# Feed-forward stages of a two-block transformer: output tiles placed between the block products, in six short stretches over a ring of eight tiles

## The reference

```
def swiglu(x, w_in, w_out):
    gate, up = jnp.split(x @ w_in, 2, axis=-1)
    return (jax.nn.silu(gate) * up) @ w_out

    x = x + FFN_HALF * rmsnorm(swiglu(rmsnorm(x, ffn1_pre_g), ffn1_w_in, ffn1_w_out), ffn1_post_g)
```

## Time and profile before

| | us |
|---|---|
| median of 2 runs | 3464.9 (3463.77 to 3466.04) |
| profiled execution, its own time | 3456.78 |
| its span in the profile | 3455.0 |

### The profile page before, as it was taken

The page is one execution under the profiler, slowest core; times in us unless marked ns, Lnnn a source line. Parts: engine busy times, 40 slices in busy tenths (PEclk is TensorE's granted clock), DMA queues, the critical chain, the costliest instruction groups (busy, mean ns, idle before and its releaser), DMA issues.

```text
span 3455.0 us, 50031 instructions
## 1 busy us (share of the span) xinstructions
PE 3112.0 (90%) x20476; PEld 2613.2 (76%) x20476; DVE 2193.9 (63%) x3116; ACT 1379.3 (40%) x2398; POOL 1493.2 (43%) x1003
## 2 busy tenths in 40 slices
PE   6999999899998989898899898997989999979897
PEld 4777778678776888876777788887888885678886
DVE  2256482446648696776554959679687616486967
ACT  3242273442454343442443434344233416452433
POOL 2234315235344474454212546427456343344743
PEclk9999999999999999998778999999999999999999
DMA  5213202212111222221001122231232230112222
GB/s 222 92 53 128 91 13 63 74 45 70 44 53 61 92 81 97 98 92 56 8 2 55 42 93 92 80 104 55 88 108 69 93 102 24 42 43 93 86 87 78
DMA packets 74164, 256.74 MB, mean 74 GB/s; under 512 B 8016, under 2 KB 11216, under 8 KB 72784
## 3 DMA queue, kind: packets, MB, share of 16 engines
q1 hardware_dynamic: 73072, 248.82, 21.3%
q0 software_dynamic: 864, 4.72, 0.4%
HBM read 251.41 MB, written 2.10 MB: 73 GB/s over the span
## 4 chain that ended last, share of the span: by engine, by line
PE 66%; DVE 19%; issue 5%; ACT 4%; POOL 4%; DMA 1%; SPq 0%; ACTq 0%; DVEq 0%; POOLq 0%
PE banks L459 64%; DVE area L1539 3%; DVE w_lo L436 3%; PE banks L468 2%; POOL w_lo L425 1%; ACT w_hi L409 1%; DVE area L1510 1%; POOL w_sum L447 1%; DVE area L1528 1%; DVE w_late L436 1%; DVE w_last L430 1%; DVE area L1517 1%; POOL w_sum L445 1%; DMA area<-in_w_mod 1%; DVE area L1534 0%
## 5 line engine op out<-in xcount | busy, mean ns | idle before, releaser
L459 PE MATMUL banks<-area,w_hi 128*128 128x256 f32 (+3 forms) x6892 | 1690.8, 337 | 154.1 <-DVE w_lo L436 120.7
L459 PEld LDWEIGHTS banks<-area,w_hi 128*128 128x128 f32 (+2 forms) x6892 | 1179.8, 191 | 335.4 <-DVE w_lo L436 134.3
L459 PE MATMUL banks<-area,w_lo 128*128 128x256 f32 (+3 forms) x3446 | 1140.8, 333 | 0.0
L459 PEld LDWEIGHTS banks<-area,w_lo 128*128 128x128 f32 (+2 forms) x3446 | 659.1, 191 | 69.8
L425 POOL TENSOR_TENSOR w_lo<-w_raw,w_hi 128x1024 fp32r<-128x1024 f32 (+2 forms) x146 | 344.8, 2363 | 517.1 <-ACT w_hi L409 479.5
L459 PE MATMUL banks<-area,w_late 128*128 128x256 f32 (+2 forms) x2766 | 499.1, 334 | 30.9 <-DVE w_late L436 29.3
L459 PEld LDWEIGHTS banks<-area,w_late 128*128 128x128 f32 (+1 forms) x2766 | 419.5, 192 | 92.7 <-DVE w_late L436 34.2
L459 PE MATMUL banks<-area,area 64*64 64x32 f32 (+11 forms) x4424 | 399.9, 314 | 65.9 <-DMA area<-in_w_mod 15.7
L459 PEld LDWEIGHTS banks<-area,area 64*64 64x64 f32 (+4 forms) x4424 | 308.7, 174 | 146.1 <-issue 57.9
L409 ACT ACTIVATE w_hi<-w_raw 128x1024 fp32r<-128x1024 f32 (+2 forms) x197 | 193.2, 985 | 321.3 <-PE banks L459 199.7
L436 DVE TENSOR_TENSOR w_lo<-w_sum,w_hi 128x1024 fp32r<-128x1024 f32 x115 | 207.1, 1803 | 47.1 <-POOL w_sum L450 42.4
(11 more groups left out here) (298 smaller groups left out, 4183.3 us busy)
## 6 DMA issues: line engine op xcount, KB each, us to landing
w_raw<-in_l_ffn_w_in SPq DMA_DIRECT2D x132, 512.0 KB, 3.4
w_raw<-in_w_in SPq DMA_DIRECT2D x66, 512.0 KB, 3.5
w_raw<-in_l_ffn_w_out SPq DMA_DIRECT2D x48, 512.0 KB, 3.5
const<-in_l_ffn_w_in SPq DMA_DIRECT2D x44, 512.0 KB, 3.5
w_raw<-in_w_mod SPq DMA_DIRECT2D x32, 512.0 KB, 4.6
w_raw<-in_w_out SPq DMA_DIRECT2D x32, 320.0 KB, 2.9
w_raw<-in_l_ffn_w_out SPq DMA_DIRECT2D x24, 384.0 KB, 3.2
w_raw<-in_w_qkv SPq DMA_DIRECT2D x18, 512.0 KB, 3.3
```

What stands on the lines that cost most here:

```text
L459: return e.matmul(out, lhsT, rhs, start=first, stop=stop, skip_group_check=True)
```

## The change

The stretches become 4, 4, 4, 4, 3, 3 tiles. The 8 output tiles of a stretch are no longer computed in a row but between the block products of the next stretch: `pairs_behind` gives each block one `w_out` piece (now two output tiles of 4 or 3 hidden tiles each; the last block of a three-block stretch has two pieces), and PE computes the first half of its output tiles between p6 and p7, the second half between p3 and p4. p4 stands in its own block. Blocks use banks 4-7 alone, output tiles banks 0-3. The hidden tiles lie in a ring of eight (`RING`). The output tiles of the last stretch follow all blocks, hidden tiles 19 and 20 first for four of them (`lead`). DVE takes out two tiles per block (`tiles_dve`), makes the rest of the `w_out` pieces between c11 and `a_lo_dve`, and takes over the rests that POOL had behind the stretches and of the first two pieces of the two mixers. ACT, DVE and POOL get the entries in a new order. The weight layout follows; the number of matmuls and bytes stays.

Lines that begin with a space stand in both kernels; "..." leaves lines out (in the ACT and DVE loops these are waits and signals).

```diff
-FFN_PHASES = ((0, 8), (8, 16), (16, 22))
+FFN_PHASES = ((0, 4), (4, 8), (8, 12), (12, 16), (16, 19), (19, 22))
+RING = 8
...
-            for p, (j0, j1) in enumerate(FFN_PHASES):
-                for c in range(2 * j0, 2 * j1):
+            for j in range(FT):
+                for c in (2 * j, 2 * j + 1):
                     yield (name + "_w_in", c, True)
-                for c in range(8):
+                for p, c in pairs_behind(j):
                     yield (name + f"_w_out{p}", c, True)
+            for c in range(4):
+                yield (name + f"_w_out{len(FFN_PHASES) - 1}", c, True)
+def pairs_behind(j):
+    p = next(p for p, (j0, j1) in enumerate(FFN_PHASES) if j0 <= j < j1)
+    if p == 0:
+        return []
+    i, n = j - FFN_PHASES[p][0], FFN_PHASES[p][1] - FFN_PHASES[p][0]
+    return [(p - 1, c) for c in range(4) if min(c, n - 1) == i]
...
-                    ents.append((n, "plain"))
-                    if ents[-2][1] == "s34":
-                        ents.append((ents[-2][0], "last"))
-                    ents += [(n, "s12"), (n, "s34")]
+                    ents += [(n, "plain"), (n, "s12"), (n, "s34"), (n, "last")]
             elif split:
-                after_units = len(ents) > 0 and ents[-1][1] == "s34"
                 ents.append((n, "whole"))
-                if after_units:
-                    ents.append((ents[-2][0], "last"))
         ent_at = {ent: k for k, ent in enumerate(ents)}
-        end_ents = {k + i for k, (n, kind) in enumerate(ents) if kind == "s34" and ents[k + 1][1] == "whole" for i in (1, 2, 3)}
...
-        last_leads = [n + i for n in firsts for i in (2, 3, 4, 5)]
+        last_leads = [n + i for n in firsts for i in range(6)]
...
-                if (kind == "whole" and dve == (("ffn" in order[m][0] or m in last_leads) and k not in end_ents)
+                if (kind == "whole" and dve == (m in last_leads or "ffn" in order[m][0])
                         or (kind == "plain" and not dve)):
...
-                if kind == "last" and dve == (k not in end_ents):
+                if kind == "last" and dve:
...
+                    final = p == len(FFN_PHASES) - 1
                     self.outs.append(ProjectOut(
-                        name, lambda m, p=p, n=j1 - j0: [(name + f"_w_out{p}", m, n)],
-                        [(self.a_hi[:, k, :], self.a_lo[:, k, :]) for k in range(j1 - j0)], T, y_sb, self.add.squares,
-                        lambda q, k, j0=j0: q.wait_ge(*at(name, "a", j0 + k)), add=p > 0, final=p == len(FFN_PHASES) - 1,
-                        free=lambda q, m, p=p: self.left_by_units(q, m, p), bank0=4 - 4 * self.bank_set(j1 - 1)))
-                assert self.outs[-1].bank0 == 0
+                        name, lambda m, p=p, n=j1 - j0: [(name + f"_w_out{p}", m // 2, n)],
+                        [(self.a_hi[:, j % RING, :], self.a_lo[:, j % RING, :]) for j in range(j0, j1)], T, y_sb,
+                        self.add.squares, lambda q, k, j0=j0: q.wait_ge(*at(name, "a", j0 + k)), add=p > 0, final=final,
+                        lead=[(m, k) for m in range(4) for k in range(j1 - j0 - 1)] if final else (),
+                        free=None if p else self.left_by_pieces, base=lambda m, n=j1 - j0: m % 2 * n))
...
-                return banks[self.quarter_bank(u, i)][:, 0:T // 2]
...
+                return banks[4 + i][:, 0:T // 2]
...
             def quarter_free(self, q, u, i):
...
+                if u > DIRECT:
                     q.wait_ge(*at(self.tag, self.LEFT_BY[i], u - 1))
...
                 else:
                     q.wait_ge(*at(self.tag, "x", "log", 0))
+            def tiles_behind(self, u, half):
+                tiles = [(p, m) for p, c in pairs_behind(u) for m in (2 * c, 2 * c + 1)]
+                n = len(tiles) // 2
+                return tiles[n:] if half else tiles[:n]
...
+                steps = [out.steps(q, e) for out in self.outs]
+                for u in range(DIRECT, FT):
+                    for name in ("p1", "p2", "p5", "p6"):
+                        self.product_pe(q, e, u, name)
+                    self.tiles_pe(steps, u, 0)
+                    for name in ("p7", "p3"):
+                        self.product_pe(q, e, u, name)
+                    self.tiles_pe(steps, u, 1)
+                    self.product_pe(q, e, u, "p4")
+                self.outs[-1].pe(q, e, steps[-1])
+            def tiles_pe(self, steps, u, half):
+                for p, m in self.tiles_behind(u, half):
+                    for _ in self.outs[p].k_tiles:
+                        next(steps[p])
...
+                if u >= RING:
+                    q.wait_ge(*at(*self.outs[self.phase(u - RING)].finished()))
+                e.activation(self.a_hi[:, u % RING, :], self.a[u % 2], ACT.Copy).then_inc(
...
+                for u in range(DIRECT, FT):
...
+                    e.activation(self.p1[u % 2], self.quarter(u, 0), ACT.Copy).then_inc(
...
+                    if u > DIRECT:
+                        self.a_hi_act(q, e, u - 1)
+                    else:
+                        for v in (0, 1):
+                            self.silu_act(q, e, v)
...
+                    e.activation(self.u2[u % 2], self.quarter(u, 0), ACT.Copy).then_inc(
...
+                    round_one(q, e, self.ent(u, "last"))
+                    if u == DIRECT:
+                        for v in (0, 1):
+                            self.a_hi_act(q, e, v)
+                        self.silu_act(q, e, 2)
+                    elif u + 1 < FT:
+                        round_one(q, e, self.ent(u + 1, "plain"))
+                    if u + 1 < FT:
+                        round_one(q, e, self.ent(u + 1, "s12"))
+                    else:
+                        round_one(q, e, self.last_ent())
+                    if u == DIRECT:
+                        self.a_hi_act(q, e, 2)
+                    self.silu_act(q, e, u)
+                    if u + 1 < FT:
+                        round_one(q, e, self.ent(u + 1, "s34"))
+                        for k in self.tile_ents(u + 1):
+                            round_one(q, e, k)
+                    else:
+                        round_one(q, e, self.last_ent() + 1)
+                self.a_hi_act(q, e, FT - 1)
+                self.final_act(q, e)
+            def after_ents(self):
+                return range(self.last_ent() + 4, ahead(ents[self.last_ent() + 3][0]) + 1)
+            def final_act(self, q, e):
+                out, after = self.outs[-1], list(self.after_ents())
+                q.w = self.last_ent() + 2
+                e.preload_act_table_set("natural_log_exp_and_others")
+                round_to(q, e, self.last_ent() + 3)
+                for k in after[:2]:
+                    round_to(q, e, k)
+                for m in range(DT - 1):
...
+                    out.squares.square(q, e, 0, m, out.y[:, m, :])
+                    if m >= 3:
+                        for k in after[m - 1:m]:
+                            round_to(q, e, k)
+                out.squares.last(q, e, 0)
...
+            def tiles_dve(self, q, e, u, half):
+                for p, m in self.tiles_behind(u, half):
+                    self.outs[p].evict(q, e, m, 0)
             def dve(self, q, e):
                 self.direct_dve(q, e)
...
+                for u in range(DIRECT, FT):
...
+                    if u > DIRECT:
+                        self.up_dve(q, e, u - 1)
+                        self.tiles_dve(q, e, u - 1, 1)
...
+                    e.tensor_tensor(self.half(sg, 0), self.quarter(u, 1), self.p1[u % 2], ADD).then_inc(
...
+                    for k in self.tile_ents(u):
+                        rest_one(q, e, k, dve=True)
+                    if u > DIRECT:
+                        self.a_lo_dve(q, e, u - 1)
+                        rest_one(q, e, self.ent(u, "s34"), dve=True)
...
+                    e.tensor_tensor(self.u4[u % 2], self.quarter(u, 2), self.u2[u % 2], ADD).then_inc(
...
+                    if u == DIRECT:
+                        rest_one(q, e, self.ent(u, "last"), dve=True)
+                        self.third_dve(q, e)
+                    self.tiles_dve(q, e, u, 0)
...
+                    e.tensor_tensor(self.half(a, 1), self.quarter(u, 3), self.u4[u % 2], ADD).then_inc(
...
+                    if u > DIRECT:
+                        rest_one(q, e, self.ent(u, "last"), dve=True)
+                    if u == DIRECT:
+                        self.product_dve(q, e, 2)
+                        rest_one(q, e, self.ent(u + 1, "s12"), dve=True)
+                        self.a_lo_dve(q, e, 2)
+                    self.gate_dve(q, e, u)
+                    if u + 1 < FT and u > DIRECT:
+                        rest_one(q, e, self.ent(u + 1, "s12"), dve=True)
+                    if u + 1 == FT:
+                        rest_one(q, e, self.last_ent(), dve=True)
+                        rest_one(q, e, self.last_ent() + 1, dve=True)
+                self.up_dve(q, e, FT - 1)
```

(24 more changed lines are left out.)

174 lines of the change are left out of this document (46 added, 128 removed).

## The result

| | before | after |
|---|---|---|
| median, us | 3464.9 (3463.77 to 3466.04, 2 runs) | 3338.35 (3338.05 to 3338.65, 2 runs) |
| ratio, 95% interval | | 0.9635 [0.9593, 0.9676] |
| span of the profiled execution | 3455.0 | 3336.3 |

The kernel became 126.6 us faster; 109 were forecast.

A forecast was written before the change was run, and what follows sets the result against it. DVE was taken to limit the block stretches, with 192 us of PE waiting. Gains of 100 us in the four stages and 9 at three borders, 109 in all, took 3464.9 to 3356 us; range 3300 to 3440.

The forecast's parts named there:

- DVE limited the block stretches, and mixing frees PE: Block stretches: DVE is the limit, costing PE 192 us of waiting; output tiles between products make PE the longer one.
- Per block 0.6 us of waiting: Blocks 5 to 18: a 16.0 us loop from p6 to the next first output tile exceeds PE's 15.4; bounds 0 and 2.3.
- DVE per block 13.6 of 15.4: One-piece blocks: DVE needs 11.0 plus two evictions and a piece's rest, 13.6 us, against PE's 15.4.
- Rival 1: Blocks: DVE stays the limit, with 1.2 to 2.3 us of waiting per block; 3423 us in all; chance 0.18.
- Start: 9.51 idle + 8.7 = 18.2 us: Stage start: PE idles 9.51 us before p5 of block 3, then blocks 3 and 4 lose 8.7 us together.
- The 4.7 for p4: Block 3: p4 waits 4.7 us for c22, which stands in DVE's queue behind `third_dve`.
- `direct_dve` before it is the same: Stage start: `direct_dve` before p5 of block 3 is unchanged, where PE idles 9.51 us.
- Blocks 19 to 21: 2.0 + 4.0: Block 19 waits 2.0 us for its late up piece; blocks 20 and 21 wait 2.0 each, PE's 14.0 against 16.0.
- Final tiles: 1.3: Last eight output tiles of a stage: two banks are free late, costing 1.3 us.
- Border: 9 us gained: Three stage borders: evictions come before the rests and POOL only adds, so 3 us are gained at each.
- Rival 3: PE is never short, as buffers two deep absorb every late chain; 3293 us; chance 0.10 (over 145 us gained).
- Rival 2: Slower: POOL holds piece rests and `a` rests, 2.7 us waiting per block; 3482 us; chance 0.12 including anything beyond.

The follow-up runs named there:

- experiment 3: Kernel before with five stretches of 6, 5, 5, 3, 3 hidden tiles and no output tiles between block products: 3502.53 us, ratio 1.0103.
- experiment 1: Changed kernel with interleaved output tiles leaving out one or two of their three matmuls: 3285.18 us with two thirds kept, 3297.87 us with one third.
- experiment 2: Changed kernel with DVE computing the rest of each `w_out` piece of the first five stretches twice: 3395.02 us, ratio to before 0.9789.
- experiment 4: Changed kernel with POOL's rest of t 3 moved behind its sums at each stage start, then also held until the lead products are done: 3331.04 and 3328.71 us.
- experiment 5: Changed kernel with DVE's last three rests of each stage held until POOL's last addition of squares: 3336.87 us, ratio 0.9629.

## Why the prediction was right, and where not

**DVE limited the block stretches, and mixing frees PE.** Right. The middle blocks lost nearly all their waiting, and experiment 3 shows that splitting alone doesn't do it. Mixing came together with p4 in its own block, one bank set, the ring and new orders of the queues; no run has these without the mixing. The Trainium skill, page "Perfetto Trace Analysis", section "Optimization Strategy", says that interleaving regimes whose most contended engine differs may improve performance. The runs agree (126.6 us) as far as PE's work exceeds the longest chain; experiment 1 shows where it ends.

**Per block 0.6 us of waiting, "I take the upper value, rounded to 16.0".** This is the term that was mis-sized. Measured: 0.0 to 0.1 per block from block 5 to 17, since the chain to the piece's rest is 15.2 us long and PE gets there at 15.2. The place was named rightly (PE waits for the piece's rest as soon as its own work is shorter), but the length was off, and the sum took it for a chain that closes in each block. By PE's order it doesn't: the piece's rest is needed only behind p6. I used the means of scaling, product and rest from the stretches in which POOL ran beside DVE most of the time (1.34, 1.66, 1.71). In the new order, of the chain's instructions behind the sums, only the rest of s12 (2.30) meets POOL: 6.2 us where I had 7.5. Against that stood a step that I missed: DVE's rest of s12 waits for POOL's fourth sum, 1.56 us more of POOL, beside which ACT's rounding (1.04 in my sum) is hidden, so 0.5 net. 14 x 0.55 x 4 = 31 us too little gain.

**DVE per block 13.6 of 15.4.** Measured 12.33. The row from which I took 11.0 held instructions stretched by POOL. Rival 1, which built on 88% load, fell with it; even a load of 79% can limit (experiment 2), but by way of the chain.

**Start: 9.51 idle + 8.7 = 18.2 us.** Measured 20.2 to 20.8 up to block 4's first output tile, right in size and wrong in make-up: in stage 1, 7.70 for the rest of s12, 6.24 for u4, 0.87 for p4, the remaining 5.4 mostly at a low clock (0.50 in the 2.5 us behind the first wait). The 4.7 for p4 shrank to 0.87 because u4's wait, which I had not seen, came first; experiment 4 brought p4's back at 3.54. The line "`direct_dve` before it is the same" is the failed step: DVE's list is the same, but what POOL does beside it isn't.

**Blocks 19 to 21: 2.0 + 4.0.** Measured in stage 1: 0.5 at block 18, 1.7 at 19, 0.4 at 20 and 0.6 at 21. At 19 the wait stood before the first output tile (1.12, for the piece's rest) and not at the rest of s12. The forecast also counted 14.0 us of PE's work for block 21; as the last of a three-block stretch it has two pieces, so 9.8 + 8.4 = 18.2, more than the 16.0 of the loop. Why block 20, with 14.0, waited so little was not tried. **Final tiles: 1.3**, measured about 0.4.

**Border: 9 us gained.** Wrong: 0.7 lost. There were two faults. I took 1453.0 for the end of the last matmul, where it is the start of the last tile's halves; their matmuls went from 36 to 18, so 2.1 us less stand between E and the addition, and all of it was eaten. And POOL's additions run 1.7 us each beside DVE's rests, where I took 1.3 (in the kernel before, three took 5.17 together and a later one 1.26):

```profile
1418.73 10.05 POOL L533 TENSOR_TENSOR area<-area,area 128x512 f32<-128x512 f32 x6 [27.30 <-ACT area L518]
```

```profile
1428.83 1.76 PE L468 MATMUL banks<-area,const 128*128 128x256 f32 x4 [2.66 <-POOL area L533]
1433.12 1.22 PE L468 MATMUL banks<-area,w_apart 128*128 128x256 f32 x4 [2.53 <-ACT area L728]
```

Both waits of PE were shorter in the kernel before: 1.04 us in front of the sum of squares, and in front of `w_apart`, here at stage 2's border:

```profile
2309.38 0.74 PE L459 MATMUL banks<-area,w_apart 128*128 128x256 f32 x4 [1.48 <-ACT area L719]
```

The queue that the change empties was not the longest. By experiment 5 the rests beside POOL cost some 1.5 us of it; the rest of the chain of additions, PE and ACT was not tried further.

**What was not in the sum: 10.1 us ahead of S.** A part of it is TensorE's clock behind the border. The 10 us behind stage 2's first addition, before and after:

```profile
2307.80:2317.80 10.00, 8.36 (x63) 7.78 (x63) 8.32 (x21) 5.12 (x14) 0.00 (x0) 1.00 0.02 8
```

```profile
2248.20:2258.20 10.00, 8.48 (x45) 8.18 (x46) 6.36 (x16) 3.94 (x10) 0.00 (x0) 0.65 0.20 78
```

The granted clock is 1.00 before and 0.65 after, and 45 matmuls start instead of 63: 18 x 0.117 = 2.1 us, where the whole stretch to the next S is 2.0 us longer. At the border of stage 1 the clock is 0.78 instead of 1.00 and 55 matmuls start instead of 64, 1.1 of the 3.0 us there. The border of stage 3 looks like that of stage 2: 0.65 instead of 1.00 and 45 matmuls instead of 63 in the 10 us behind the addition, so 2.1 of the 3.8 us before stage 4. The other 1.7 may be spread, since that stretch took 348.7 to 352.3 us in the kernels made from the changed one. The 1.3 us before stage 1 are spread as well: over the kernels of this study, which don't differ there, that stretch ended at 1087.6 to 1097.0.

**The sum.** 100 + 9 forecast; 129.5 - 0.7 - 10.1 = 118.7 came. In waiting a stage won 34.5 us and not 25.1: 7.7 more in the steady blocks, some 3.7 at blocks 18 to 21 and the final tiles, about 1.3 because more waiting stood there before than I had counted, and 2.3 less at the start; 1 us of this sum is left over. The forecast came near the total because the border and the stretches ahead of S took back part of what the blocks gave beyond it: that is luck. Rival 3 (PE never short) was right in the steady blocks, which are most of the stage, and wrong at the start. Rival 2 needed 2.4 us per block; experiment 2, which lengthens the chain, reaches 0.7 with PE's work unchanged.

## What to carry to other kernels

When two kinds of work are mixed, don't stop at the engines' loads: write out the longest chain through the in-order queues from one iteration to the next, with every wait of each of its instructions, and compare it with the busiest engine's work; note too how many iterations it takes to close. DVE at 79% set the period here as soon as 1.1 us was added to its chain, and at 80% without it didn't. And take durations from neighbours of the same kind: a mean from a stretch of contention is too long for an order that pulls the rivals apart, and a code path that is unchanged can get slower when the other engine's queue next to it moves.
